# Order q, v, k, gate for the next pair's blocks, and every turn on TensorE as fp32r words

## The reference

```python
ada = silu(c) @ w_ada + b_ada;  shift, scale, gate = split(ada, 3)
h = rmsnorm(x, g_norm) * (1 + scale) + shift
q_sb, k_sb, v_sb, q_fx, k_fx, v_fx, g_path, f_logit = split(h @ w_in)
# stick breaking, strictly causal: A[t,s] = sigmoid(z_ts) * prod_{s<j<t} (1 - sigmoid(z_tj))
# forgetting, causal softmax: logit[t,s] = q_t.k_s/8 + sum_{s<j<=t} log f_j
y = concat(rmsnorm(o_sb), rmsnorm(o_fx)) * g_grp * silu(g_path)
x = x + (1 + gate) * (y @ w_out)
out = rmsnorm(x, g_final)
```

## Time and profile before

| | us |
|---|---|
| runs | 739.99, 738.69, 739.97 (median 739.97) |
| the profiled execution | 738.17 |
| its span | 736.4 |
| PE busy | 698.0 (95% of the span) |
| DVE / ACT / POOL busy | 482.4 / 423.8 / 363.5 |
| granted TensorE clock, mean | 0.993 |

### The profile page before, as it was taken

One profiled execution on the slowest core, in us unless ns is written; L12 is line 12 of the kernel. 1 busy time (PEld: TensorE's weight loads), 2 busy tenths in 40 slices (PEclk: granted clock), 3 DMA queues, 4 the chain that ended last, 5 costly groups with the idle time before them and its releaser, 6 DMA issues.

```text
span 736.4 us, 10800 instructions
## 1 busy us (share of the span) xinstructions
PE 698.0 (95%) x3830; PEld 583.6 (79%) x3830; DVE 482.4 (66%) x992; ACT 423.8 (58%) x883; POOL 363.5 (49%) x329
## 2 busy tenths in 40 slices
PE   2989988999999999999999999999999999999995
PEld 0667877788888888888888888888888888788884
DVE  4977998656655776466557764665587655555566
ACT  5875767555765655556756555567565646333222
POOL 1020464467894453688845546767566463321100
PEclk9999999999999999999999999999999999999998
DMA  9942231223342110334421102444323087882222
GB/s 353 409 158 86 66 134 32 86 100 115 130 145 89 69 42 16 101 115 144 143 91 55 48 10 86 144 162 154 107 73 101 22 279 250 278 264 87 86 115 114
DMA packets 35463, 93.14 MB, mean 126 GB/s; under 512 B 4297, under 2 KB 5961, under 8 KB 34898
## 3 DMA queue, kind: packets, MB, share of 16 engines
q1 hardware_dynamic: 28450, 73.71, 28.6%
q0 software_dynamic: 5376, 14.68, 6.2%
q10 hardware_dynamic: 1584, 4.05, 1.4%
HBM read 68.81 MB, written 23.63 MB: 126 GB/s over the span
## 4 chain that ended last, share of the span: by engine, by line
PE 77%; DVE 10%; ACT 6%; issue 3%; POOL 1%; DMA 1%; SPq 0%; DVEq 0%; ACTq 0%; POOLq 0%
PE psum L1593 12%; PE psum L1594 12%; PE psum L1601 12%; PE psum L1692 11%; PE psum L1680 8%; PE psum L1656 7%; PE psum L1625 4%; PE psum L1624 4%; DVE work L1245 3%; DVE stacks L1213 2%; DVE pt_lo L1306 1%; DMA work<-in_x 1%; PE psum L1523 1%; PE psum L1537 1%; ACT work L910 1%
## 5 line engine op out<-in xcount | busy, mean ns | idle before, releaser
L1593 PE MATMUL psum<-h_hi,w_hi 128*128 128x512 f32 x448 | 186.0, 415 | 1.9 <-DVE stacks L1213 1.9
L1594 PE MATMUL psum<-h_lo,w_hi 128*128 128x512 f32 x448 | 176.8, 395 | 0.0
L699 POOL TENSOR_TENSOR work<-work 128x127 f32<-128x127 f32 (+3 forms) x64 | 82.9, 1296 | 165.6 <-DVE work L1245 165.6
L949 ACT ACTIVATE pt_hi<-psum 128x512 fp32r<-128x512 f32 (+1 forms) x192 | 88.2, 490 | 101.6 <-PE psum L1656 98.5
L1306 DVE TENSOR_TENSOR pt_lo<-psum,pt_hi 128x512 fp32r<-128x512 f32 (+1 forms) x192 | 101.3, 553 | 58.1 <-ACT pt_hi L949 55.7
L1245 DVE TENSOR_TENSOR_SCAN work<-work 128x128 f32<-128x128 f32 (+3 forms) x64 | 95.7, 1495 | 40.6 <-ACT work L910 40.3
L1601 PE MATMUL psum<-h_hi,w_lo 128*128 128x512 f32 x448 | 120.5, 391 | 0.0
L1601 PEld LDWEIGHTS psum<-h_hi,w_lo 128*128 128x128 f32 x448 | 84.4, 188 | 18.8
L1593 PEld LDWEIGHTS psum<-h_hi,w_hi 128*128 128x128 f32 x448 | 85.1, 190 | 17.3 <-issue 2.7
L1594 PEld LDWEIGHTS psum<-h_lo,w_hi 128*128 128x128 f32 x448 | 85.0, 190 | 15.0
L1656 PE MATMUL psum<-ident,work 128*128 128x128 f32 x576 | 87.4, 277 | 6.7 <-DVE v_stack L1285 3.9
(11 more groups left out here) (186 smaller groups left out, 1331.1 us busy)
## 6 DMA issues: line engine op xcount, KB each, us to landing
w_raw<-in_w_blocks SPq DMA_DIRECT2D x30, 512.0 KB, 4.2
w_split_scratch<-work SPq DMA_DIRECT2D x16, 512.0 KB, 3.3
work<-in_x SPq DMA_DIRECT2D x12, 512.0 KB, 7.7
work<-in_w_ada_t SPq DMA_DIRECT2D x10, 512.0 KB, 7.0
y_split_scratch<-work SPq DMA_DIRECT2D x10, 512.0 KB, 3.5
v_stack_early<-in_w_ada_t SPq DMA_DIRECT2D x8, 512.0 KB, 3.3
work<-forget_scratch SPq DMA_DIRECT2D x8, 512.0 KB, 5.2
work<-in_w_out SPq DMA_DIRECT2D x16, 256.0 KB, 3.2
```

The lines of the kernel that those rows point to most:

```text
L699: nc.gpsimd.tensor_tensor(U[g % 2][:, 0:n - 1], U[g % 2][:, 0:n - 1], R[g % 2][:, 1:n], ALU.mult).then_inc(s_prob, 1)
L949: nc.scalar.activation(pt_hi[:, a:e, (g % 2) * P:(g % 2 + 1) * P], bank, ACT.Copy).then_inc(s_thi, 1)
L1593: nc.tensor.matmul(bank, hi, h_hi[:, c_, cols], start=(c_ == 0), stop=False)
L1594: nc.tensor.matmul(bank, hi, h_lo[:, c_, cols], start=False, stop=False)
```

## The change

**Order.** The next pair's blocks come as q, v, k, gate instead of q, k, gate, v. V is turned in steps 9 and 10 of the pair before (`V_NEXT`), instead of step 14 of the pair before and step 2 of its own pair; only pair 0 keeps its own (step 0 and step 2). The k parts leave in steps 9 to 11 (`K_SECOND, K_WHOLE = 10, 11`) instead of 5 to 7, the gate in 13 and 15 instead of 9 and 11.

**Turns.** `turned` is a second name, of type fp32r, for the memory of `work`, which holds x, v and the probabilities; `ident_r` is a copy of the identity in fp32r, made by DVE at the start. All 672 turns take these two and write PSUM as fp32r words. PE's first wait is for `ident_r` (`s_ones` at 3) instead of for the load of `ident`.

```diff
-            blocks += [(p + 1, "q"), (p + 1, "k"), (p, "g"), (p + 1, "v")]
+            blocks += [(p + 1, "q"), (p + 1, "v"), (p + 1, "k"), (p, "g")]
...
-    K_SECOND, K_WHOLE = 6, 7
-    V_STEPS = [STEPS - 2, 2]
+    K_SECOND, K_WHOLE = 10, 11
+
+    V_NEXT, V_FIRST = (9, 10), 2
...
+        work_at = (nc.sbuf_base + 31) // 32 * 32
         work = sb("work", [P, 9, SEQ])
+
+        turned = nc.alloc_sbuf_tensor_at("turned", [P, 9, SEQ], fp32r, offset=work_at)
...
+        ident_r = sb("ident_r", [P, P], fp32r)
...
-                if i == V_STEPS[0] and p + 1 < PAIRS:
-                    vt_out(p + 1, 0)
-                if i == V_STEPS[1]:
-                    vt_out(p, 1)
-                    if p >= 1:
-                        square_pair(p - 1)
+                if i in V_NEXT and p + 1 < PAIRS:
+                    vt_out(p + 1, V_NEXT.index(i))
+                if g == V_FIRST:
+                    vt_out(0, 1)
+                if i == 2 and p >= 1:
+                    square_pair(p - 1)
...
-                v_first = is_sb(g) and i == V_STEPS[0] - 1
-                if v_first:
-                    proj_out(u)
...
-                elif i % 2 == 1 and u < len(units) and not v_first:
+                elif i % 2 == 1 and u < len(units):
...
+            nc.vector.tensor_copy(ident_r[:], ident[:]).then_inc(s_ones, 1)
...
-            pe.wait_ge(s_id, 16)
+            pe.wait_ge(s_ones, 3)
...
-                    last = nc.tensor.transpose(bank[:, (k - a) * P:(k - a + 1) * P],
-                                               U[g % 2][:, k * P:(k + 1) * P], ident[:])
+                    last = nc.tensor.transpose(bank[:, (k - a) * P:(k - a + 1) * P].bitcast(fp32r),
+                                               turned[:, g % 2, k * P:(k + 1) * P], ident_r[:])
...
-                if i == V_STEPS[0] and p + 1 < PAIRS:
-                    transpose_v(p + 1, 0)
-                if i == V_STEPS[1]:
-                    transpose_v(p, 1)
+                if i in V_NEXT and p + 1 < PAIRS:
+                    transpose_v(p + 1, V_NEXT.index(i))
+                if g == V_FIRST:
+                    transpose_v(0, 1)
```

More of the change, by code:

```diff
@@ L120, in hybrid_trunk_kernel @@
         p, i = g // STEPS, g % STEPS
[L121 to L124, removed]
+        if i in V_NEXT and p + 1 < PAIRS:
+            t_items.append(("V", p + 1, V_NEXT.index(i)))
+        if g == V_FIRST:
+            t_items.append(("V", 0, 1))
         if g < UNITS and (p, i) == (PAIRS - 1, SUMS_AT):
@@ L1497, in turn_x @@
                 for t in range(4):
-                    last = nc.tensor.transpose(X_BANK[:, t * P:(t + 1) * P],
-                                               x_row(t)[:, d * P:(d + 1) * P], ident[:])
+                    last = nc.tensor.transpose(X_BANK[:, t * P:(t + 1) * P].bitcast(fp32r),
+                                               turned[:, t, d * P:(d + 1) * P], ident_r[:])
                 last.then_inc(s_xt, 1)
@@ L1644, in transpose_v @@
                 for k in range(4):
-                    last = nc.tensor.transpose(bank[:, k * P:(k + 1) * P],
-                                               VT[:, (4 * j + k) * P:(4 * j + k + 1) * P], ident[:])
+                    last = nc.tensor.transpose(bank[:, k * P:(k + 1) * P].bitcast(fp32r),
+                                               turned[:, 6, (4 * j + k) * P:(4 * j + k + 1) * P], ident_r[:])
                 last.then_inc(s_t, 1)
```

## The result

The changed kernel takes 726.86 us (median of four runs, 726.27 to 728.14), the kernel before 739.77 beside it: a ratio of 0.983, with an interval of 0.981 to 0.985. So 12.9 us are gone. My forecast was 31 us, and 709.0. The time lies in the range that I gave, but the gain is well under half of the forecast, and that it lies near the 730 of rival 1 is only half for rival 1's reason.

The account below looks back on a forecast made before the run. PE was taken to be bound by its own throughput. Gains A to D, 37.0 us, less losses E and F, 6.0, gave 31.0 net: 707.2 by the profile, 709.0 by the median; range 700 to 731, this case's own 701 to 716.

Parts of the forecast that it names:

- rival 1: Load holds an fp32r turn at 0.11 us, so turns save nothing: 729.9 (chance .13) or 736.3 us (.09).
- A: PE's turns as fp32r: each takes 0.061 us instead of 0.109, in pairs, v and x; saves 23.9 us.
- B: PE's stalls at v's turns, such as step 14, go: 3.9 us recorded plus 7 x 0.18 hidden, 5.2 us.
- C: PE's waits for DVE's k parts and for a bank in pair 0 go, as k parts leave the wide scans: 4.3 us.
- D: Pair 0's values: PE's wait for low parts behind DVE's forget scan and the half clock after it go: 3.6 us, if all goes.
- E: Loss because POOL is late with probabilities for a faster PE: SB step 3 0.7, FX step 2 0.7, pair 5 1.1 us.
- SB step 3: POOL's probabilities come 0.24 us late for PE in each of three SB pairs, 0.7 us lost in all.
- FX step 2: POOL's probabilities come 0.23 us late for PE in each of three FX pairs, 0.7 us lost in all.
- Pair 5 with its 18 jobs: POOL has 18 extra jobs in pair 5 and only 0.17 us slack; 1.1 us lost in its last steps.
- F: Loss because DVE is late: pair 0 1.5 us, SB steps 9 to 11 1.0, unseen ACT and queues 1.0.
- What I could not see: Part of the loss F: 1.0 us for ACT and queues that the prediction could not see.
- off go 22: 22 turns in steps 4 to 7 of pair 7 excluded from A's saving, because the chain there runs over ACT and DVE.

Follow-up runs that it names:

- split_later: Changed kernel with POOL's two low parts of the first weight block of an SB pair moved behind step 3's probabilities; 724.34 us, 0.9805 of the kernel before.
- two_mends: Changed kernel with last-pair x loads behind w_out's parts and, in pairs 2, 4, 6 only, POOL's split behind step 3's probabilities; 721.09 us, 0.9773 of before.
- turn_forms: Changed kernel plus 96 unread turns and plain products of six forms at PE's end; fp32 turn 0.109 us, fp32r 0.087; with 64 columns 0.063 and 0.083.
- fx_split_too: two_mends with POOL's first-block split also behind the probabilities of step 2 in forgetting (FX) pairs; 720.44 us, 0.9761 of the kernel before.
- order_only: Kernel before with only the change's new order, keeping the old fp32 turns; 732.69 us, 0.9925 of the kernel before.

## Why the prediction was wrong

**The reading of the bound was right.** PE is bound by its work; the edits that took PE's waits away in split_later and two_mends gave back what the steps said.

**A. The step that failed.** I took 0.061 us for an fp32r turn "since the transpose mode stays and the words' length stays". That is an argument from names: the earlier trace rows shows the load of an fp32 turn, and I carried it over. (Its second load starts 0.01 us after the first turn, not ahead of it; the 0.06 is borne out by turn_forms.) The turn is 0.086, held not by its stream (turn_forms) but, as what is left, by its load. It is the term that was mis-sized, not its sign or its mechanism. The stream does fall below the load, as I said. By the size of the groups the 448 turns gave about 7.2 us where I had 21.5. The distance alone, 0.109 less 0.086, would be 0.023 for each instead of 0.048, so 10 us; but a single fp32r turn is 0.05 slower than a single fp32 one (16 of them, 0.8), and most groups gave 0.02 to 0.03 less than their distances. With v and x it is about 9 where I had 23.9: 15 of the 19 us that are missing (31.0 less the 11.9 of the two profiled spans). I had given the "upper end ... 0.11 or a little more" and no row between the ends; 0.086 lies in the middle, and the rival with 0.11 was so near to the time because the order was worth less as well.

What the Trainium skill's "TensorE: Matmul & The Clock Gate", section LDWEIGHTS, says of a load, P/1.2 ns, 107 for 128 columns, is confirmed for plain products (0.11) and for neither kind of turn (0.063 and 0.086).

**B held.** V's waits are gone, 1.05 us in step 14 of an SB pair and 0.28 in that of an FX pair, 5.0 in all where I had 5.2. That a recorded wait hides 0.18 us more was needed for it.

**C and D.** The k parts and the bank gave 3.6 us where I had 4.3 (pairs 2, 4, 6: 0.56, 0.76, 0.42; pair 0: 0.79 and 1.08). In pair 0's steps 10 and 11 the order alone gave 0.7 (0.25 and the 0.44 that v's turns added) + 1.4 = 2.1 where I had 3.6: the half clock is gone, as forecast, and behind the forget scan v's low part took the place of pt_lo's, with 1.3 us. The window that answers to that of the earlier trace rows:

```profile
124.00:127.00 3.00, 2.95 (x15) 2.18 (x13) 2.89 (x6) 2.62 (x6) 3.00 (x3) 1.00 0.00 0
```

This term was sized "if all goes", and I had named DVE as full there; I should have asked which item comes next behind that scan.

**E, the right place with the wrong size.** I expected POOL late in SB step 3, by 0.24 us, from slack against slack. It was 1.35. The slack counted on a multiplication of 1.09 us, and the mechanism that made it 2.27 stood in the kernel before. These rows, of pair 0 in steps 10 and 11, I had not read; POOL, then DVE:

```profile
128.76 3.54 POOL L699 TENSOR_TENSOR work<-work 128x511 f32<-128x511 f32 x2
...
128.08 2.07 DVE L1245 TENSOR_TENSOR_SCAN work<-work 128x640 f32<-128x640 f32 x1
```

The same 3.54 for the same two instructions, with a scan begun before them. A look at whether one form has two durations, and beside what, would have given 1.2 us for each of three pairs.

The Trainium skill has the rule, in "SBUF — State Buffer", section "SBUF: two separate sides": DVE and GpSimd share one pair of ports, under an exclusive lock that whichever instruction starts first holds to its end; DVE's with two inputs from SBUF take it against a GpSimd instruction that reads SBUF, and the other is blocked entirely. The runs agree: 511 columns begun in a scan took 2.27, begun before one 1.09, and the one PSUM reader on DVE that ran beside POOL's work cost it nothing. Blocked to the scan's end, the 511 columns would have taken 1.38 + 1.09 = 2.47, so some 0.2 us of an instruction pass in the wait. It holds the other way round as well: the scan that began while POOL multiplied took 1.96 us in the kernel before, and 1.50 in split_later, where POOL had 0.14 left. I had not looked it up, and it speaks against this change at that place.

FX step 2 was right (0.2 us each, 0.23 got back by fx_split_too). Pair 5 with its 18 jobs, for which I had taken 1.1, lost nothing that its neighbours didn't.

**F.** Pair 0 gave back less than the 1.5: the turns' saving shows in all its steps but 7 and 11. The 1.0 for steps 9 to 11 of the SB pairs came to 0.2 (order_only: 0.07 in each of pairs 2, 4 and 6 above the 0.44 of v's turns).

What I could not see was for 1.0 and came to more, in step 5 of pair 7. Steps 4 to 7 of pair 7 were on my list as an ACT chain "off go 22", with nothing lost; between order_only and the changed kernel they lost 1.0 net instead of gaining 0.4. Two things meet there. The larger is the half clock, which the kernel before does not have in this pair: 3.4 us of it in order_only, 6.8 in the changed kernel. The smaller is the transfer of w_out's parts. It is not that PE comes earlier to it, for PE wants the parts 14.4 us after their issue, and in the kernel before 14.6; but they land 15.2 us after it instead of 11.4 (14.2 in order_only). The three loads of y that POOL issues ahead of them now land 1.9 to 3.4 us later, counted from that issue.

So of the 19 missing us A has 15, E's step 3 has 3.3 (4.1 less the 0.7 of my sum), D 1.5, C 0.7, B 0.2 and pair 7 some 1.4, of which up to 1.1 comes and goes with the length of its half clock. Against these stand some 4 that did not come: 1.1 for pair 5, 1.0 of the 1.5 for pair 0, 0.8 for steps 9 to 11, and the 1.0 for what I could not see, which is pair 7's own. That makes 18; for the last one no run here shows a place.

## What to carry to other kernels

Where the duration of a new form of instruction is the largest term of a sum, it is a term with two ends and no middle: the forecast should say what the time is at both, and the range of the likeliest case should hold them, not only its own. Before an instruction is taken away from an engine that isn't the bound, look at what comes earlier for it and beside what that will run; a form that has two durations in the trace is the sign.

## What the runs showed of the hardware

- A turn (transpose with 128 rows) starts every 0.109 us with fp32 words and every 0.086 with fp32r words at full clock; with 64 columns streamed 0.063 and 0.083. The loads: 0.063 and at most 0.086. A plain fp32r product starts every 0.11 to 0.12 at full clock, and at the lower level every 0.21 with 128 columns as with 64. A single fp32r turn is 0.05 us slower than a single fp32 one.
- An fp32 multiplication or subtraction of POOL that begins while a scan of DVE from memory to memory is running takes about as much longer as the rest of the scan: 511 columns 2.27 instead of 1.09 us (1.38 of it beside the scan), 512 columns 2.47 instead of 1.30. One that began first keeps its 1.09 (the scan begins 0.49 later). A scan begun while POOL multiplies is longer as well (1.96 instead of 1.50). DVE's low part, which reads PSUM, left POOL's time alone (1.30 against 1.29).
- The clock in pair 7: at 1.2 GHz for 3.4 us in six and 6.8 us in five of the eleven profiles of edited kernels, never in that of the kernel before. One program shows both lengths, and the longer one makes pair 7 about 1 us longer.
- The clock after the short turns of turn_forms (PE never idle between), windows: length, busy times, granted clock, DMA share, GB/s:

```profile
725.30:726.70 1.40, 1.40 (x20) 1.36 (x18) 0.00 (x0) 0.00 (x0) 0.00 (x0) 1.00 0.04 12
726.80:730.00 3.20, 3.20 (x19) 3.20 (x19) 0.00 (x0) 0.00 (x0) 0.00 (x0) 0.58 0.00 0
730.00:733.00 3.00, 3.00 (x16) 3.00 (x16) 0.00 (x0) 0.00 (x0) 0.00 (x0) 0.50 0.00 0
733.00:736.00 3.00, 3.00 (x8) 2.42 (x9) 0.00 (x0) 0.00 (x0) 0.00 (x0) 0.50 0.00 0
```

It fell to 1.2 GHz without any wait of PE, after 32 turns of 64 columns and in the midst of plain products of 128, and stayed there through eight products of 512 columns.
